# Routing an expert layer on the raw residual, with one expert's place fixed: a two-layer decoder trunk on one core

## What is computed

```python
hn = rmsnorm(h, norm_ffn[1])                      # h / rms(h) * gain
logits = hn @ w_router                            # 256 x 8
top_vals, top_idx = lax.top_k(logits, 2)
gates = softmax(top_vals)
for e in range(8):
    g, u = split(hn @ w_gu[e])                    # 1024 x 5632
    y += combine[:, e] * ((silu(g) * u) @ w_down[e])   # 2816 x 1024
h = h + y
h = h + sigmoid(rmsnorm(h, norm_ple[1]) @ w_ple_gate[1]) * (p[1] @ w_ple_up[1])
```

## Time and profile before

| | |
|---|---|
| median of 3 runs (lowest, highest) | 1200.89 us (1199.78, 1202.69) |
| the profiled execution | 1198.75 us, span of the core 1196.8 us |
| mean granted TensorE clock | 0.97 |
| TensorE busy | 1128.6 us (94%) |
| DVE, ACT busy | 301.9 us, 219.2 us |
| DMA through SyncE's queue | 342.74 MB |

### The profile page before, as it was taken

How to read it: one execution, slowest core, us unless ns; L and a number is a source line. 1 busy time by engine, 2 the same in 40 slices (tenths; PEclk the granted TensorE clock), 3 DMA queues, 4 the chain that set the end, 5 groups by cost and what they waited for, 6 DMA issues and landing times.

```text
span 1196.8 us, 21470 instructions
## 1 busy us (share of the span) xinstructions
PE 1128.6 (94%) x9605; PEld 624.4 (52%) x9606; DVE 301.9 (25%) x528; ACT 219.2 (18%) x342; POOL 9.4 (1%) x52
## 2 busy tenths in 40 slices
PE   7887999999999987999999999999999999999958
PEld 5556999997487444344334343353353343343326
DVE  4664554453324432000100100100100101001042
ACT  2362434433214410000000000000000000000033
POOL 2000000000000000000000000000000000000000
PEclk9888999999999996999999999999999999999979
DMA  9805655552120006999999999999999999999920
GB/s 321 306 1 176 211 176 179 201 185 106 36 106 1 1 1 260 420 416 419 419 418 414 417 419 419 417 419 419 406 400 348 417 419 419 418 419 418 404 117 35
DMA packets 114170, 344.15 MB, mean 288 GB/s; under 512 B 7774, under 2 KB 30875, under 8 KB 114075
## 3 DMA queue, kind: packets, MB, share of 16 engines
q1 hardware_dynamic: 114074, 342.74, 72.8%
HBM read 341.67 MB, written 1.05 MB: 286 GB/s over the span
## 4 chain that ended last, share of the span: by engine, by line
PE 91%; DVE 5%; ACT 2%; DMA 1%; issue 1%; DVEq 0%; ACTq 0%
PE ps L1739 34%; PE ps L1790 12%; PE ps L1515 6%; PE ps L1516 6%; PE ps L1517 6%; PE ps L1499 5%; PE ps L1795 4%; PE ps L1720 3%; PE ps L1635 2%; PE ps L1575 1%; PE ps L1763 1%; PE ps L1808 1%; DMA wring<-in_w_ple_gate 1%; PE ps L1390 1%; PE ps L1365 1%
## 5 line engine op out<-in xcount | busy, mean ns | idle before, releaser
L1739 PE MATMUL ps<-wring,xg 128*32 128x512 f32 (+1 forms) x4704 | 417.8, 503 | 2.2 <-DVE e_h L1240 1.4
L1739 PEld LDWEIGHTS ps<-wring,xg 128*32 128x32 f32 x4704 | 156.1, 110 | 244.0 <-issue 199.9
L1790 PE MATMUL ps<-wring,ehT 128*32 128x512 f32 x1408 | 165.2, 599 | 11.0 <-DVE ehT L1252 11.0
L1515 PE MATMUL ps<-dn_high,w_high 128*128 128x256 f32 x352 | 100.7, 286 | 2.5 <-DVE dn_low L1088 2.5
L1790 PEld LDWEIGHTS ps<-wring,ehT 128*32 128x32 f32 x1408 | 44.7, 111 | 109.5 <-issue 108.2
L1516 PE MATMUL ps<-dn_low,w_high 128*128 128x256 f32 x352 | 100.5, 285 | 0.0
L1517 PE MATMUL ps<-dn_high,w_low 128*128 128x256 f32 x352 | 100.4, 285 | 0.0
L1079 DVE TENSOR_TENSOR w_low<-ring,w_high 128x2048 fp32r<-128x2048 f32 x33 | 75.5, 2291 | 58.4 <-ACT w_high L676 58.4
L778 ACT COPY ehT<-ps 128x384 f32<-128x384 f32 (+1 forms) x24 | 10.5, 439 | 372.1 <-PE ps L1763 258.8
L1252 DVE COPY ehT<-ps 128x384 f32<-128x384 f32 (+3 forms) x24 | 10.8, 449 | 256.6 <-PE ps L1763 187.4
L1515 PEld LDWEIGHTS ps<-dn_high,w_high 128*128 128x128 f32 x352 | 68.5, 194 | 3.3 <-DVE dn_low L1088 2.9
(11 more groups left out here) (284 smaller groups left out, 964.7 us busy)
## 6 DMA issues: line engine op xcount, KB each, us to landing
wring<-in_w_exp_gu SPq DMA_DIRECT2D x128, 1024.0 KB, 17.4
wring<-in_w_exp_down SPq DMA_DIRECT2D x88, 1024.0 KB, 15.6
wring<-in_w_exp_gu SPq DMA_DIRECT2D x64, 768.0 KB, 14.6
ring<-in_w_ffn_gu SPq DMA_DIRECT2D x44, 512.0 KB, 5.2
ring<-in_w_ffn_down SPq DMA_DIRECT2D x11, 1024.0 KB, 5.1
ring<-in_w_ple_gate SPq DMA_DIRECT2D x4, 1024.0 KB, 4.8
ring<-in_w_q_b SPq DMA_DIRECT2D x4, 1024.0 KB, 4.9
ring<-in_w_o_b SPq DMA_DIRECT2D x4, 1024.0 KB, 6.3
```

The lines of the kernel that those rows point to most:

```text
L1515: pe.matmul(out, high_l, high_r, start=first, stop=False)
L1739: return pe.matmul(ps[32 * quarter:32 * quarter + 32, bank, c0:c0 + 2 * nf * P], xg[:, k, 32 * b:32 * b + 32], w[:, :, f * P:(f + nf) * P] ...
L1790: ins = pe.matmul(ps[32 * q:32 * q + 32, 3, :], turned(g, 2 * u + r, b, nb), w[:, r, half * 512:(half + 1) * 512], start=(g == 0 and u == ...
```

## The change

- TensorE transposes the raw residual `h`, without norm factor and gain; the router weights are multiplied by the gain once, before attention. The logits so lack the token's positive norm factor, which the ranking doesn't need; it enters where the gates are computed (`gates`, scale of the exponential). The sum of squares, the root and `hs` = h x root (now on ACT, without gain) are made beside it. The gain is multiplied in where DVE copies the gathered rows to `xg`. ACT copies one half of the transposed tile, DVE the other.
- Expert 7 (`FIRST`) always has the first turn. Its LEAD units are loaded without waiting for the order, seven as soon as ring slots come free, nine after the output projection. Its load is raised by 1024 for the ranking (and its room too), and its picks come straight from `slot_of`. `gates` and `order_experts` run after its gathered rows. Its two gathers use banks 3 and 4.
- The second embedding's weights come at the end of the front's loads; its products are cut in four quarters (`embedding`) and placed between the routing steps of TensorE; ACT copies the results to `up1`, where the last step reads them.
- The last gate's four units are loaded before the last expert's `down` 1 and 2, to other places; the raw and split parts are laid out anew. TensorE reads the largest overflow before the last expert's last groups.
- The 512 KB load of the gain, spread over partitions, is left out.

The diff, cut to its core (constants that shift the slot numbers by one, declarations and memory places are left out):

```diff
+FIRST = E - 1
+PINNED = 1024.0
...
+    place.update({("end",) + u: place[("alone",) + u] for u in alone})
+    place.update({("end", "down", 1, u): 1024 * 11 + 2048 * u for u in range(4)})
+    place.update({("end", "down", 2, u): 1024 * 19 + 2048 * u for u in range(3)})
...
-    free["end"] = [*free["body"][:16], 24, 25, 26]
+    free["end"] = [*free["body"][:12], 15, 16, 17, 18, 19, 20, 21]
...
-        sp_.dma_start(ffn_gain[:, :], a["norm_ffn"][1:2, :].to_broadcast([P, D])).then_inc(ffn_gain_in, 16)
...
-        sp_.wait_ge(order_done, 1)
-        e = sp_.value_load(expert_at[0:1, 0:1], min_val=0, max_val=E - 1)
-        for name, g, u in LEAD:
-            expert_dma(sp_, "lead", name, g, u, e)
+        sp_.dma_start(up1[:], rows(a["w_ple_up"][1], 0, 2)).then_inc(up1_in, 16)
+        for k, (name, g, u) in enumerate(LEAD):
+            if k < 7:
+                sp_.wait_ge(*released(*order[45 + k]))
+            elif k == 7:
+                sp_.wait_ge(o_b_ready, NT)
+            expert_dma(sp_, "lead", name, g, u, FIRST)
+        e = FIRST
         for n in range(E - 1):
+            if n == 0:
+                sp_.wait_ge(order_done, 1)
...
-        loads("alone", ALONE, E - 1, lambda i: e, "end")
-
-        def tail_loads(p):
-
-            for i, (name, u) in enumerate(tail):
-                sp_.wait_ge(e_used, p * EUNITS - (EUNITS - used_count("alone", "down", 0)))
-                src = rows(a["w_ple_up"][1], 0, 2) if name == "ple_up1" else rows(a["w_ple_gate"][1], 2 * u, 2 * u + 2)
-                sp_.dma_start(tail_view(i), src).then_inc(t_landed[i], 16)
-
-        tail_loads(E)
+        def gate_loads(p, last_pass):
+
+            for u in range(4):
+                sp_.wait_ge(e_used, p * EUNITS - (EUNITS - 11 - u) if last_pass else p * EUNITS)
+                dst = wring[:, 1024 * (3 + 2 * u):1024 * (5 + 2 * u)].rearrange("p (k n) -> p k n", k=2)
+                sp_.dma_start(dst, rows(a["w_ple_gate"][1], 2 * u, 2 * u + 2)).then_inc(t_landed[u], 16)
+
+        down_at = ALONE.index(("down", 1, 0))
+        loads("end", ALONE[:down_at], E - 1, lambda i: e, "end")
+        gate_loads(E, True)
+        loads("end", ALONE[down_at:], E - 1, lambda i: e, "end", down_at)
...
-        norm(4)
-        for t in range(NT):
-            act.wait_ge(top_done, t + 1)
-            act.activation(gexp[:, t, :], lg[:, t, :], ACT.Exp, bias=ntop[:, t:t + 1]).then_inc(gexp_done, 1)
+        for t in range(NT):
+            act.wait_ge(h_updated, 6 + t + 1)
+            act.wait_ge(sq_done, NT * 4 + t)
+            act.activation(junk[:], h[:, t, :], ACT.Square, accum_out=sumsq[:, 4, t:t + 1]).then_inc(sq_done, 1)
+            act.wait_ge(hT_done, 4 * 4 + 2 * t + 2)
+            act.copy(hnT[:, 4:8, t * P:(t + 1) * P], ps[:, norm_bank(4, t) + 1, :].rearrange("p (c n) -> p c n", c=4)).then_inc(hnT_done, 1)
+        for t in range(NT):
+            rsqrt_seed(r_norm(4, t), rstd[:, 4, t:t + 1])
+        for t in range(NT):
+            act.wait_ge(rstd_ready, t + 1)
+            act.mul(hs[:, t, :], h[:, t, :], rstd[:, 4, t:t + 1]).then_inc(hs_done, 1)
 
         def used(kind, name, g, n):
             c = used_count(kind, name, g)
             act.wait_ge(e_used, EUNITS * n + c if isinstance(n, int) else n * EUNITS + c)
+
+        act.wait_ge(up1_ready, 4)
+        for t in range(NT):
+            for half in range(2):
+                act.copy(up1[:, t, half * 512:(half + 1) * 512], ps[:, 4 + 2 * t + half, :]).then_inc(up1_done, 1)
+        for t in range(NT):
+            act.wait_ge(top_done, t + 1)
+            act.activation(gexp[:, t, :], lg[:, t, :], ACT.Exp, bias=ntop[:, t:t + 1], scale=rstd[:, 4, t:t + 1]).then_inc(gexp_done, 1)
...
-                act.wait_ge(t_landed[1 + k // 2], 16 * (1 + again))
-                act.wait_ge(e_used, p * EUNITS - (EUNITS - len(LEAD) - (4 if k < 3 else 6 if k < 6 else 12)))
-                act.mul(gate_high(k), gate_raw(k), gainT[:, G_PLE + 8 + k:G_PLE + 9 + k]).then_inc(t_high, 1)
+                act.wait_ge(t_landed[k // 2], 16 if last_pass else 32)
+                act.wait_ge(e_used, p * EUNITS - (14 - (1, 1, 2, 3, 3, 4, 5, 5)[k]) if last_pass else p * EUNITS)
+                act.mul(gate_high[:, k], gate_raw(k), gainT[:, G_PLE + 8 + k:G_PLE + 9 + k]).then_inc(t_high, 1)
...
+        dve.wait_ge(wr_in, 16)
+        dve.tensor_tensor(wr[:], wr[:], bc(gainT[:, G_FFN + 8:G_FFN + 16].unsqueeze(2), [P, KD, E]), ALU.mult).then_inc(wr_ready, 1)
...
-        norm(4, None, add_to_h(o_b_ready), early=True)
-
-
-        for t in range(NT):
+        add_attention = add_to_h(o_b_ready)
+
+        def half_turned(t):
+            dve.wait_ge(hT_done, 4 * 4 + 2 * t + 1)
+            dve.tensor_copy(hnT[:, 0:4, t * P:(t + 1) * P], ps[:, norm_bank(4, t), :].rearrange("p (c n) -> p c n", c=4)).then_inc(hnT_done, 1)
+
+        def find_top(t):
+
             dve.wait_ge(lg_ready, t + 1)
             link(dve.tensor_copy(lg[:, t, :], ps[:, t, 0:E]))
-            dve.tensor_reduce(top[:, t:t + 1], lg[:, t, :], AX.X, ALU.max).then_inc(top_found, 1)
-            other = bc(lg[:, t, :].unsqueeze(1), [P, E, E])
+            other = bc(ps[:, t, 0:E].unsqueeze(1), [P, E, E])
             own = bc(lg[:, t, :].unsqueeze(2), [P, E, E])
             dve.tensor_tensor(cmp_gt[:, t], other, own, ALU.is_gt)
             link(dve.tensor_tensor(cmp_eq[:, t], other, own, ALU.is_equal))
-            dve.wait_ge(top_found, t + 1)
-            dve.tensor_scalar(ntop[:, t:t + 1], top[:, t:t + 1], -1.0, None, ALU.mult).then_inc(top_done, 1)
             link(dve.tensor_tensor(cmp_eq[:, t], cmp_eq[:, t], earlier[:], ALU.mult))
             link(dve.tensor_tensor(cmp_gt[:, t], cmp_gt[:, t], cmp_eq[:, t], ALU.add))
             link(dve.tensor_reduce(rank[:, t, :], cmp_gt[:, t], AX.X, ALU.add))
             dve.tensor_scalar(picked[:, t, :], rank[:, t, :], 2.0, None, ALU.is_lt).then_inc(picked_done, 1)
 
-        dve.wait_ge(gexp_done, NT)
+        add_attention(0)
+        half_turned(0)
+        add_attention(1)
+        find_top(0)
+        half_turned(1)
+        for t in range(NT):
+            dve.wait_ge(sq_done, NT * 4 + t + 1)
+            means(r_norm(4, t), ((sumsq[:, 4, t:t + 1], D),))
+        for t in range(NT):
+            r = rstd[:, 4, t:t + 1]
+            if t:
+                dve.wait_ge(rstd_ready, t)
+            dve.tensor_tensor(r, r, correction(r_norm(4, t), r), ALU.mult).then_inc(rstd_ready, 1)
+        find_top(1)
...
+            link(dve.tensor_scalar(load[:, FIRST:], load[:, FIRST:], PINNED, None, ALU.add))
...
-            for src, dst in ((slot_of, turn_slot), (gate, turn_gate)):
+            for src, dst in ((gate, turn_gate), (slot_of, turn_slot)):
...
-                if dst is turn_slot:
-                    turn_picks(0)
...
-            dve.tensor_copy(xg[:, 4 * half:4 * half + 4, 0:32 * nb], ps[:, 7, 0:4 * 32 * nb].rearrange("p (k n) -> p k n", k=4)).then_inc(e_xg_done, 1)
+            b = (3 + half) if isinstance(k, int) and k == 0 else 7
+            f = G_FFN + 8 + 4 * half
+            dve.tensor_tensor(xg[:, 4 * half:4 * half + 4, 0:32 * nb], ps[:, b, 0:4 * 32 * nb].rearrange("p (k n) -> p k n", k=4),
+                              bc(gainT[:, f:f + 4].unsqueeze(2), [P, 4, 32 * nb]), ALU.mult).then_inc(e_xg_done, 1)
...
-        order_experts()
+        picks(lambda t: slot_of[:, t, FIRST:], 0, 0, TILES[0])
         for half in range(2):
             gathered(0, half, TILES[0])
+        gates()
+        order_experts()
         product(0, 0, TILES[0])
...
-                link(dve.tensor_tensor(sig1[:, t, cols], sig1[:, t, cols], ps[:, (0, 1, 2, 7)[2 * t + half], :], ALU.mult))
+                link(dve.tensor_tensor(sig1[:, t, cols], sig1[:, t, cols], up1[:, t, cols], ALU.mult))
...
+        def turn_residual(t):
+
+            pe.wait_ge(h_updated, 6 + t + 1)
+            for half in range(2):
+                for c in range(4):
+                    k = 4 * half + c
+                    ins = pe.transpose(ps[:, norm_bank(4, t) + half, c * P:(c + 1) * P], h[:, t, k * P:(k + 1) * P], ident[:])
+                ins.then_inc(hT_done, 1)
+
+        project_tile("o_b", 1, 2, oTB, KD, o_b_ready, k0=4, k1=6)
+        turn_residual(0)
+        project_tile("o_b", 1, 2, oTB, KD, o_b_ready, k0=6)
+
+        def embedding(t, half):
+
+            for c in range(2):
+                ins = pe.matmul(ps[:, 4 + 2 * t + half, :], pT[:, 1, c, t * P:(t + 1) * P], up1[:, c, half * 512:(half + 1) * 512],
+                                start=(c == 0), stop=(c == 1))
+            ins.then_inc(up1_ready, 1)
+
+        pe.wait_ge(wr_ready, 1)
         for t in range(NT):
             if t:
-                turn_tile(4, t)
+                pe.wait_ge(up1_in, 16)
+                embedding(0, 0)
+                turn_residual(t)
+                embedding(0, 1)
             wait_turned(4, t)
             for k in range(KD):
```

(20 more changed lines are left out.)

138 lines of the change are left out of this document (67 added, 71 removed).

## The result

| | before | after |
|---|---|---|
| median (lowest to highest), 4 runs each | 1200.34 us (1199.24 to 1202.69) | 1171.40 us (1170.94 to 1172.06) |
| the profiled execution | 1198.75 us, span 1196.8 | 1171.78 us, span 1169.7 |

The ratio is 0.9757, 95% interval 0.974 to 0.9774. The forecast was 1174.5 us with a range of 1165 to 1184. The two profiled executions differ by 27.0 us; the sum was 26.4.

What follows compares the result with a forecast made beforehand. TensorE was taken to bound the expert stage's middle, leaving gains before and after: routing 13.4 + middle 0 + tail 13.0 = 26.4 us, from 1198.75 to 1172.3, plus 2.1 for the median: 1174.5 us, range 1165 to 1184.

Steps and rivals of the forecast that it cites:

- The bound of the middle: Middle of the expert stage: TensorE sets the pace, with DMA close behind; the change gives 0 us there.
- Rival 3: Expert stage: DMA bounds all of it, so early weights give 27 us less, 1147 us; chance 0.03.
- The turn of the second tile: Start of routing: second token tile's transposes and router products end at 445.7 instead of 449.3 us, gain 3.6 us.
- Counts and picks: Routing after the router products: counts end at 448.6, picks at 449.7, first gather starts at 451.1 us, 7.2 us earlier.
- Gathers and the first expert: End of routing: gathers without waits, products start at 455.1 us, 12.1 earlier; first 192 products 1.3 us shorter.
- Routing: From the second tile's turn through the first expert's first products: 13.4 us gained in all.
- Rival 1: Routing: TensorE's clock stays low there, costing about 11 us, 1185.5 us; chance 0.14.
- The last expert: Its last two groups: TensorE waits for weights but ends at 1146.5 instead of 1153.0 us, gain 6.5 us.
- Rival 2: Last expert: gate weights loaded in front hold nothing up, 1168.3 us; chance 0.12.
- The last gate: After the last expert: embedding products gone 5.1, transposes 1.1, slower first gate products -0.5, earlier register load 0.8 us.
- rival 4: Fixed expert choice overflows its places: two more passes, over 190 us slower, near 1370 us; chance 0.01.
- The tail: Last expert and last gate together: 6.5 + 5.1 + 1.1 - 0.5 + 0.8 = 13.0 us gained.

Runs made afterwards that it cites:

- norm_on_path: The changed kernel, with the second tile's transposes waiting until square, root and scaling of both tiles are done: 1173.31 us, ratio 0.9781.
- quarters_later: The changed kernel, with the second embedding's four quarters moved out of routing to behind the first expert's group 0: 1179.88 us, ratio 0.9822.
- copy_at_three: The changed kernel, with ACT copying the embedding's first quarter out of PSUM when three quarters are done, not four: 1170.91 us, ratio 0.9765.

## Why the prediction was right

- **The bound of the middle** was TensorE. Its wait list has no wait on weights there, and holding back 16 units cost 13.4 us, not 40. Rival 3, the rule of the Trainium skill (Perfetto Trace Analysis, Identifying the Most-Contended Engine) read as "DMA is the bound", is out: weight loads filled only 40% of the middle, and still TensorE set the end.
- **The turn of the second tile**: 3.6 us forecast; the second router products end at 445.3 instead of 449.3 us, 4.0. From the start of the first router products it is 7.9 us instead of 11.7; the other 0.2 us lay before. The 3.7 us divide: 1.8 us are the norm off the path, as `norm_on_path` shows, and 1.7 us the second router products at full clock (1.85 us instead of 3.58).
- **Counts and picks**: the count products end at 448.3 (forecast 448.6), the picks at 449.3 (449.7), the gathers start at 451.00 (451.1). ACT's copy was the last thing awaited, as the sum had it.
- **Gathers and the first expert**: products at 454.72 (455.1), first 192 in 20.81 us (21.0). Routing gave 12.5 + 1.5 = 14.0 us, 13.4 forecast. The multiplication by the gain was covered, as costed: for the second half it took 0.56 us at 454.82, beside the first products, which wait for the first half only.
- **The clock** was 1.00 in all windows of routing. Rival 1 was wrong for the reason given against it; `quarters_later` shows that without the embedding's quarters its low clock would have come.
- **The last expert**: the last product ends 20.5 - 13.9 = 6.6 us earlier relative to the work before it, 6.5 forecast. The reading of the wait list was wrong in part. I took ACT for the cause and not the DVE copy that the list names; the splits and the late gate weights were the cause, but they held both engines, and DVE's copy ended last, 1.4 us behind ACT's. It did no harm to the sum, because the change brings the gate weights forward for both. Rival 2 was wrong: five waits on expert units came, 4.2 us, where I had 6, and the last unit was there at 1130.6 us (1131.3).
- **The last gate**: transposes another 4.9 us earlier (5.1 + 0.8 forecast), the gate's products 1.7 us (1.1 - 0.5). The first was over-sized: the register load gave its microsecond, but the jump took 1.2 us more than the earlier trace rows, with a second transfer of instructions in it. The second was under-sized: 16 transposes took 3.5 us instead of 4.0, and the gate's first products did not run slow. That was luck: in `copy_at_three`, whose tail is the same program, they did, and from there to the end it took 1.1 us longer.
- **Overflow** (rival 4) did not occur; the 73 tokens of expert 7 fit.

The tail so gave 13.2 us for 13.0, the whole 27.1 us of span for 26.4. That the tail comes so close is luck in part: two misses of 1 us, the jump and the last gate's clock, cancel. Of the 3.1 us between 1174.5 and 1171.4 us, 0.5 lie in the profiled execution (1171.78 for 1172.3). The rest is the offset between it and the median: I had added 2.1 us, and after the change the median lay 0.4 us below the profiled execution. The chances given add up to 1.01.

## What to carry to other kernels

Where a shared resource looks full beside an engine that looks full, the engine's wait list decides, and holding transfers back tells what they are worth. In a stretch of short dependent steps, independent products put into the gaps can cost less than nothing, because idle time also costs the clock of what follows. When a transfer is moved in a queue, list for each engine the work that becomes ready with it: here the order on ACT and DVE held TensorE for 11 us, and with that mended DVE's 15 us of queue became the limit. Where two engines hang on one late transfer, the wait list names the one that ended last, and both have to be mended.

## What the hardware showed that I had not expected

- Routing with 7 us less work for TensorE took 1.2 us longer. With idle stretches of 1.1 to 1.7 us between short products the clock was 0.50 from 440 to 450 us, and behind one of 2.63 us the gathers took 1.6 us longer. In the changed kernel, with pauses of 0.5 to 1.8 us between groups of 16 products of the last expert, it was 1.00 from 1115 to 1135 us.
- One jump of TensorE over code that isn't run took 3.4 to 5.0 us in kernels that differ little, and repeated within 0.1 us in the same kernel. Where one transfer of 16 KB of instructions ran in it, it took up to 3.9 us; where two ran, 4.7 us or more.
